# Down-projection weights of the experts fetched through ScalarE's DMA queue instead of SyncE's

## What is computed

```python
def grouped_moe(x, w_router, b_router, w_up, w_down):
    ...
    xs = x_pad[slot_tok].reshape(n_blocks, M, D)
    def expert_block(args):
        xb, e = args
        a, g = jnp.split(xb @ w_up[e], 2, axis=-1)
        return (jax.nn.silu(g) * a) @ w_down[e]
    ys = lax.map(expert_block, (xs, block_expert)).reshape(P, D)
    out = jax.ops.segment_sum(ys * slot_gate[:, None].astype(ys.dtype), slot_tok,
                              num_segments=T + 1)[:T]
    ...
```

## Time and profile before

| What | Value |
|---|---|
| median of 3 runs | 1707.38 us |
| the profiled execution's own time | 1705.15 us |
| its span, first to last instruction | 1703.4 us |
| granted TensorE clock, mean | 0.966 |
| PE busy, share of the span | 1583.9 us, 93% |
| DVE | 1166.2 us, 68% |
| ACT | 833.3 us, 49% |
| DMA moved over the span | 329.27 MB, mean 193 GB/s |
| up pairs fetched, each 1024 KB | 128 |
| down pairs fetched, each 1024 KB | 64 |

### The profile page before, as it was taken

The page is one execution under the profiler, slowest core; times in us unless marked ns, Lnnn a source line. Parts: engine busy times, 40 slices in busy tenths (PEclk is TensorE's granted clock), DMA queues, the critical chain, the costliest instruction groups (busy, mean ns, idle before and its releaser), DMA issues.

```text
span 1703.4 us, 20254 instructions
## 1 busy us (share of the span) xinstructions
PE 1583.9 (93%) x7646; PEld 1315.7 (77%) x7646; DVE 1166.2 (68%) x1348; ACT 833.3 (49%) x1125; POOL 238.0 (14%) x277
## 2 busy tenths in 40 slices
PE   7999999999999999999998982799999999999990
PEld 6788888888888888887887872588888888877770
DVE  3755868586666665423754548599999999888874
ACT  3113111216555554334311111588888888878765
POOL 0000000202122210000000220022221211222220
PEclk8999999999999999999999995899999999999995
DMA  4144535654234311411733544799999999999965
GB/s 156 40 90 65 124 74 83 80 109 122 75 100 119 94 51 64 147 44 47 242 121 132 197 147 165 288 369 375 378 367 355 362 352 349 356 353 363 341 229 208
DMA packets 156869, 329.27 MB, mean 193 GB/s; under 512 B 15805, under 2 KB 85437, under 8 KB 156776
## 3 DMA queue, kind: packets, MB, share of 16 engines
q1 hardware_dynamic: 140888, 289.70, 52.6%
q0 software_dynamic: 15888, 38.31, 7.4%
HBM read 296.75 MB, written 48.50 MB: 203 GB/s over the span
## 4 chain that ended last, share of the span: by engine, by line
PE 83%; DMA 9%; DVE 4%; ACT 2%; issue 0%; SPq 0%; POOL 0%; POOLq 0%; DVEq 0%; ACTq 0%
PE ps L714 52%; PE ps L986 22%; DMA e_raw<-in_w_up 4%; DMA e_raw<-in_w_down 4%; PE ps L815 2%; PE ps L800 2%; DVE e_lo L1735 2%; PE ps L993 1%; PE ps L953 1%; DMA x_raw<-in_x 1%; ACT zsq L1336 1%; PE ps L999 1%; ACT zsq L1332 0%; PE ps L945 0%; DMA xg<-x_d,tok_i 0%
## 5 line engine op out<-in xcount | busy, mean ns | idle before, releaser
L1735 DVE TENSOR_TENSOR e_lo<-e_raw,e_hi 128x1024 fp32r<-128x1024 f32 x376 | 436.6, 1220 | 43.2 <-ACT e_hi L1274 39.7
L1274 ACT ACTIVATE e_hi<-e_raw 128x1024 fp32r<-128x1024 f32 x376 | 368.6, 1051 | 38.8 <-DMA e_raw<-in_w_down 28.0
L714 PE MATMUL ps<-xt_hi,w_hi 128*128 128x512 f32 x896 | 303.7, 395 | 2.4 <-DVE xt_lo L1368 2.4
L714 PE MATMUL ps<-xt_lo,w_hi 128*128 128x512 f32 x896 | 299.4, 391 | 0.0
L714 PE MATMUL ps<-xt_hi,w_lo 128*128 128x512 f32 x896 | 299.3, 391 | 0.0
L714 PEld LDWEIGHTS ps<-xt_hi,w_lo 128*128 128x128 f32 x896 | 168.7, 188 | 36.0
L714 PEld LDWEIGHTS ps<-xt_hi,w_hi 128*128 128x128 f32 x896 | 168.6, 189 | 35.2 <-DVE xt_lo L1368 2.6
L714 PEld LDWEIGHTS ps<-xt_lo,w_hi 128*128 128x128 f32 x896 | 169.1, 189 | 33.2
L1401 DVE TENSOR_TENSOR w_lo<-w_raw,w_hi 128x512 fp32r<-128x512 f32 x136 | 95.0, 704 | 131.6 <-ACT w_hi L1059 128.2
L1059 ACT ACTIVATE w_hi<-w_raw 128x512 fp32r<-128x512 f32 x136 | 83.6, 628 | 201.1 <-PE ps L714 199.6
L986 PE MATMUL ps<-e_hi,xe_hi 128*128 128x512 f32 x512 | 162.9, 399 | 13.3 <-DVE e_lo L1735 10.9
(11 more groups left out here) (273 smaller groups left out, 2292.3 us busy)
## 6 DMA issues: line engine op xcount, KB each, us to landing
e_raw<-in_w_up SPq DMA_DIRECT2D x128, 1024.0 KB, 21.5
e_raw<-in_w_down SPq DMA_DIRECT2D x64, 1024.0 KB, 21.9
w_raw<-in_w_in SPq DMA_DIRECT2D x64, 256.0 KB, 4.9
w_raw<-in_w_gate SPq DMA_DIRECT2D x48, 256.0 KB, 3.6
gates_d<-gate_t POOLq DMA_DIRECT2D x16, 512.0 KB, 3.6
gate_s<-gates_d SPq DMA_DIRECT2D x16, 512.0 KB, 3.7
qkv_d<-qkv POOLq DMA_DIRECT2D x12, 512.0 KB, 3.9
w_raw<-in_w_branch SPq DMA_DIRECT2D x24, 256.0 KB, 3.7
```

The costliest lines, as they stand in the source:

```text
L714: last = nc.tensor.matmul(o(h, c1 - c0), st(k), mv(k, c0, c1), start=start and k == nk[0] and n == 0, stop=h in stop and k == nk[-1] and n ...
L1274: nc.scalar.activation(e_hi[:, (UPT + s) % RSPL, :], e_raw[r][:, s % 2, :], ACT.Copy).then_inc(e_h, 1)
L1735: nc.vector.tensor_tensor(e_lo[:, sp_, :], e_raw[raw_slot(b, s)][:, s % 2, :], e_hi[:, sp_, :], ALU.subtract).then_inc(e_all, 1)
```

## The change

SP's static list leaves out the down pairs from pair 14 on. ACT gets a function `fetch_down` that issues them on its own DMA queue: for blocks 4 to 30 two blocks ahead, after its splits s = 6 and s = 8 (the pairs of block 3 likewise in step 1), and those of step 2 (pairs 14 and 15) after the splits s = 4 and s = 6 of block 0. Each keeps the same wait for a free slot. 58 transfers move. The up pairs, the first 14 pairs and all of the dynamic part (`fetch_of`) stay with SP.

```diff
             for k in range(RRAW, item(STATIC, 0) // 2):
-                fetch(k)
+                if (k + 2) % (XT // 2) < UPT // 2:
+                    fetch(k)
...
+            def fetch_down(b, i):
+
+                k = item(b, UPT + 2 * i) // 2
+                act.wait_ge(e_all, 2 * (k - RRAW + 1))
+                nc.scalar.dma_start(e_raw[k % RRAW][:], w_down[0, b - 1, 2 * i * P:(2 * i + 2) * P, :].rearrange("(k p) n -> p k n", p=P)
+                                    ).then_inc(eraw_in[k % RRAW], 16)
+
...
             def step(b):
                 for s in range(XT):
                     split(b, s)
+                    if isinstance(b, int) and b + 2 < STATIC and s in (6, 8):
+                        fetch_down(b + 2, s // 2 - 3)
...
             for s in range(4, UPT):
                 split_first(s)
+                if s in (4, 6):
+                    fetch_down(2, s // 2 - 2)
```

## The result

| | before | after |
|---|---|---|
| median | 1707.38 us (1706.37 to 1708.38, 5 runs) | 1716.64 us (1714.0 to 1717.37, 5 runs) |
| the profiled execution's own time | 1705.15 us | 1714.0 us |
| its span | 1703.4 us | 1712.4 us |
| start of PE's last group of 24 matmuls | 1656.31 us | 1665.31 us |

The ratio is 1.0049, with a 95% interval of 1.0037 to 1.0062: slower by 8.4 us (6.3 to 10.6). The forecast was +5.0.

A forecast was written before the change was run, and what follows sets the result against it. DMA delivery of expert weights was taken to bound the late experts' stage (3.20 us a pair against PE's 2.95). All terms were 0 except +5.0 us on the tail: 1705.15 to 1710.15, plus 2.23 to the median, 1712.4 us; range 1700 to 1724.

The forecast's parts named there:

- Down pairs overtake and up pairs pay: Experts' stage, two queues: about four down pairs land early, up pairs run about 13 us later than in one queue.
- Starvation begins: Experts' stage: PE starts to lack weights near 1360 us instead of 1460, and on up pairs.
- loss of delivery: Experts' stage, fewer weights landed in total; the prediction said the total delivered does not change.
- The start: Pairs 14 and 15, issued by ACT 12 us and more later, still land before use: 0 us.
- The wait that comes with the issue: ACT's wait for DVE after splits s=6 and s=8: 0.3 us on DVE, 0 in sum, bound 9 us.
- ACT's issue: 58 issues on ACT at 0.37 us each: 0 on the path, 0.74 us a block without ACT's idle time.
- the sum on the tail: End of the experts' stage: up pair 181 lands last, 182 and 183 lie ready; +5.0 us, bounds +2 to +8.
- the order of landing: Main case, experts' stage: down pairs land early, up pairs late, costing time at the end; 1709 to 1716 us, chance 0.48.
- rival 3: ACT held 2.6 us in each issue, as SP is, in the experts' stage: 1728 us, chance 0.14.
- nothing to see: Queues share in another way, or the last up pair lands earlier: 1705 to 1710 us, chance 0.20.
- Faster: Two queues make a weight pair cheaper than 3.20 us: down to 1697 us, typically 1702, chance 0.18.

The follow-up runs named there:

- e12_waits: Changed kernel with all weights in SP's queue in the old order; ACT makes the 58 waits but issues nothing: 1707.64 us.
- e10_spread_act: Changed kernel plus one router line that spreads a block's gathered tokens over partitions 0, 2, 4 and so on, then 1, 3, 5: 1694.5 us.
- e9_spread: Kernel before the change plus one router line that spreads a block's gathered tokens over partitions 0, 2, 4 and so on, then 1, 3, 5: 1694.48 us.
- e11_dot: Changed kernel with all weights in SP's queue in the old order; ACT makes the 58 waits and issues 0.5 KB at each: 1708.72 us.
- e14_own14: Changed kernel, but from block 14 on ACT issues both down pairs 4 pairs ahead of use, not 14: +0.3 us against the kernel before.
- e5_early: Changed kernel, but ACT issues only the down pairs of blocks 2 to 15 (28 transfers), SP the rest: 1709.72 us.
- e2_second: Changed kernel, but ACT issues only the second down pair of each of blocks 2 to 30 (29 transfers): 1709.53 us.
- e6_late: Changed kernel, but ACT issues only the down pairs of blocks 24 to 30 (14 transfers), SP the rest: 1714.02 us.
- e4_swap: Changed kernel the other way round: ACT issues the up pairs from pair 16 on (112 transfers), SP keeps the down pairs: 1717.51 us.
- e3_later: Changed kernel, but ACT issues every down pair one step later, 8 pairs ahead of use, from the first block on: 1717.9 us.
- e13_later14: Changed kernel, but from block 14 on ACT issues both down pairs 8 pairs ahead of use, not 14: +2.4 us against the kernel before.
- e1_small: Changed kernel with all weights in SP's queue in the old order; ACT makes the 58 waits and issues 4 KB at each: 1710.65 us.

## Why the prediction was right in sign and short in size

**What held.** Down pairs overtake and up pairs pay: landings of 12.8 and 31.5 us, as forecast under 20 and over 22. Starvation begins at 1345 us, on up pairs (forecast 1360). The last static pair lands as early as before, at 1627.94 us against 1628.30 (forecast 1628.3), so loss of delivery is not the price. The start cost nothing (309 GB/s at 1060 to 1110 us, before 297). The wait that comes with the issue is on DVE 0.5 us at its s = 7 (forecast 0.3), and e12_waits shows it free. ACT's issue lasts 0.37 us. In the timeline of after, wait and issue together do take engine time, as the split behind them starts 1.01 us after the one ahead ended:

```profile
1185.32 0.37 ACTq L1281 DMA_DIRECT2D e_raw<-in_w_down  x1
1185.79 1.06 ACT L1275 ACTIVATE e_hi<-e_raw 128x1024 fp32r<-128x1024 f32 x1 [1.01 <-DVE e_lo L1747]
...
1186.88 1.22 DVE L1747 TENSOR_TENSOR e_lo<-e_raw,e_hi 128x1024 fp32r<-128x1024 f32 x1 [0.47 <-ACT e_hi L1275]
```

but a block still costs PE 17.73 us early in the stage (transposes from 1103.50 to 1280.83 us, ten blocks), against 17.69.

**What failed is one term, the sum on the tail**, +5.0 us, in two of its assumptions. It took the last landing, up pair 181, for the last pair that PE is short of, and said that just two down pairs, 182 and 183, would lie there. The landing itself came when it was forecast, but PE wasn't there yet. PE's last gap ended at 1615.07 us, ahead of pair 174, and the last pair that ACT waited for was 175, split from 1615.14 us, 13 us earlier than the forecast's 1628.3. At that moment four down pairs lay ready, 176, 177, 182 and 183, and the up pairs 178 to 181 landed at 1620.4, 1622.9, 1625.4 and 1627.9, 2.5 us apart, quicker than the 2.95 us at which PE eats. The two pairs 176 and 177 gave these ups the time to land. From pair 175 on there was nothing to wait for, and nothing to win either: from 1615.07 on PE had ten pairs to do, 29.8 us, up to 1644.9, and then the whole of block 31. The forecast had three pairs left at 1630.6 and so reached the same point, which answers before's 1634.70, at 1639.7. It came 10.2 us after before's, where +5.0 was forecast. Before was itself starved a little in block 31 (ACT waited 1.3 us for pair 189), so that 1.2 of that were won back: +9.0 at the last group, which ends at 1671.07 and not at 1667.1.

DMA's side of it is the stretch of 1600 to 1630 us. Each digit is the share of the 16 DMA engines in tenths, 0.75 us a slice; after, then before:

```profile
DMA  9999999999997779994655322211111114752000
```
```profile
DMA  9999999999999989997543222239499999999999
```

In after the share falls from 1613.5 us on and is 10 to 20% from 1619.5 to 1624.8: two or three engines' worth of sixteen, on the rest of the last up pairs. A pair is there only when its last part is: of pair 174's 16 completions the first came at 1589.9 us and the last at 1612.67, and its split began at 1612.69. The kernel before fills this from 1618.9 us on with block 31's transfers, whose waits hang on DVE's progress; after, DVE is late and they begin at 1630.18. I read the capacity that lies unused while PE is behind as the other side of the loss; no run fills it, so that isn't shown. The bounds of the term, +2 to +8, allowed for one pair's price either way; the miscount was of two pairs (2 x 2.95 us, against the 5.2 us that the point came late), and 8.4 lies just outside.

The median, 1716.64 us, lies in the range of 1700 to 1724, but 0.6 us above the 1709 to 1716 that the order of landing had. The range's room above that came from rival 3, ACT held up, which did not happen in this change. So that the range held is in part luck. Two slips in the forecast's working change nothing: an item is six matmuls, so that two items are 12 in all (the 2.74 us are right), and 14.8 + 2 x 2.6 is 20.0, not 20.1.

Of the rivals, "nothing to see" falls by the ratio. The Trainium skill (DMA: Bandwidth & Descriptors, Issuing engines are not separate DMA queues) was cited for it: issuing from several engines saves sequencer time only. e10_spread_act beside e9_spread agrees, since the time is the same there (1694.5 and 1694.48 us) and so is the rate at 1253 to 1458 us (382 and 383 GB/s). Where DMA sets the pace the measurement decides: the order of landing changed, 12.8 and 31.5 us in place of 22, and the kernel became 8.4 us slower. "Faster" falls by the rates, 376 and 354 GB/s: two queues did not make a pair cheaper. "ACT held up" falls for this change by the issues of 374 ns.

**What stays open:** whether e11_dot's 58 tiny transfers cost more (2.2 us) than e14_own14's 58 large ones (0.3). Their intervals share 0.7 to 1.9, and the medians lie 1.3 and 0.9 us above before's, so no difference is shown. Open too are the 2.7 us of e5_early, and how much of the tail's price each of the last down pairs carries: e2_second's seven late ones cost next to nothing, e6_late's fourteen 7.7 us.

## What to carry to other kernels

When transfers are split over two queues, the one with less ahead of it is served sooner, and what it gains the other pays; here this was free while DMA had room and cost time once it had none, above all at the end of the stage. There, find the last moment at which the consumer was short, count what lies ready then, and let no transfer lead by more than it needs: 14, 8 and 4 pairs of lead cost 8.4, 2.4 and 0.3 us. But while DMA has room leave no slot empty: shortening the lead from the start on, and not from block 14, cost 8.7 us more. And before reordering a starved queue, ask why it is slow: here a line that spreads the rows of other transfers was worth -13.7 us.

## What the runs showed of the hardware

- Landing time is set by the latest of a transfer's 16 completions. In before, 8 of pair 74's came 5.2 to 6.6 us after its issue and the others at 12.6 to 19.6; of pair 160's, issued when the queue was full, 12 came by 9.9 us and the last four at 14.1 to 22.3. With the gathered tokens spread over the partitions a pair lands in 11.8 us instead of 22 (e9_spread). That the gathers and scatters of 64 rows on low partitions load a part of the 16 DMA engines more than the rest is the reading of these numbers; the load of single engines was not measured.
- A full queue holds only the engine that issues to it: SP stood up to 8.0 us in an issue while ACT's took 0.374 us in the same stretch; ACT stood up to 3.27 us in its own when the up pairs went there, and SP's took no longer than usual (e4_swap).
- PE's last group of 24 matmuls comes behind an idle time of 2.2 to 4.3 us. It took 5.7 to 5.8 us in before, after, e3_later and both spread kernels, 7.2 to 7.4 in seven others (e2_second, e6_late, e13_later14 and e14_own14 among them), and 8.5 and 8.6 in e1_small and e5_early. In the slower ones the granted clock was at the level of 1.2 GHz, not 2.4, for 3.4 us around the group's start, in the last two for 6.8. The stretch of 1662 to 1666 us in e2_second, then in after, whose group starts at 1665.31:

```profile
1662.00:1666.00 4.00, 4.00 (x12) 3.09 (x11) 0.00 (x0) 0.00 (x0) 0.15 (x1) 0.57 0.47 70
```
```profile
1662.00:1666.00 4.00, 1.76 (x10) 1.28 (x9) 2.70 (x3) 1.61 (x3) 1.13 (x1) 1.00 0.00 0
```

  A single profile so carries 1.6 to 2.9 us of chance in its end, and 2.6 us in where the experts' stage starts (1068.3 to 1070.9 us). The start of the last group is a better mark than the end, and small differences need the timed medians.
